# Moving the SBUF buffer of the weights' high parts by 384 bytes

## What is computed

```python
# first block, one layer
u = modulate(h, ...);  y = (silu(u @ w_gate) * (u @ w_up)) @ w_down   # d_ff 2816
h = layer_norm(ALPHA * h + 0.5 * gate * y)
u = modulate(h, ...);  y = hybrid_token_mixer(u, w_in, ...)          # conv, SSM, attention
h = layer_norm(ALPHA * h + gate * y)
... # the same feed-forward a second time, with other weights
# second block, one layer
z = rmsnorm(x) @ w_in;  ...                                          # attention, mLSTM
x = x + mixed @ w_out
u = relu(rmsnorm(x) @ w_ff1);  x = x + (u * u) @ w_ff2               # d_ff 4096
```

## Time and profile before

| | |
|---|---|
| median of 3 runs | 2522.7 us (2516.86 to 2528.89) |
| profiled execution | 2523.61 us |
| its span, first to last instruction | 2521.6 us |
| mean granted TensorE clock | 0.990 |
| PE, PEld, DVE, ACT, POOL busy | 97%, 92%, 74%, 51%, 43% |
| DMA | 481.35 MB, mean 191 GB/s |

### The profile page before, as it was taken

One profiled execution on the slowest core, in us unless ns is written; L12 is line 12 of the kernel. 1 busy time (PEld: TensorE's weight loads), 2 busy tenths in 40 slices (PEclk: granted clock), 3 DMA queues, 4 the chain that ended last, 5 costly groups with the idle time before them and its releaser, 6 DMA issues.

```text
span 2521.6 us, 52685 instructions
## 1 busy us (share of the span) xinstructions
PE 2448.4 (97%) x20017; PEld 2309.8 (92%) x20017; DVE 1872.2 (74%) x2869; ACT 1279.5 (51%) x2099; POOL 1077.4 (43%) x618
## 2 busy tenths in 40 slices
PE   7999999999999999999999999999999999999999
PEld 4999999878989989999998788999989999989999
DVE  5875999677687687679996777776856676756776
ACT  3445456356554454444553665544654544654544
POOL 3434987312043333369871110433650344740444
PEclk9999999899999999999999999999999999999999
DMA  9885864333477677767643235875434556534564
GB/s 365 302 287 186 276 222 135 114 106 104 151 279 255 191 261 277 251 233 243 201 135 101 93 101 191 285 256 170 138 123 143 171 188 191 169 103 149 172 188 133
DMA packets 131496, 481.35 MB, mean 191 GB/s; under 512 B 14848, under 2 KB 14848, under 8 KB 130560
## 3 DMA queue, kind: packets, MB, share of 16 engines
q1 hardware_dynamic: 106992, 388.49, 47.4%
q0 software_dynamic: 23040, 83.90, 9.1%
q10 hardware_dynamic: 1296, 6.64, 0.7%
HBM read 475.82 MB, written 3.15 MB: 190 GB/s over the span
## 4 chain that ended last, share of the span: by engine, by line
PE 71%; DVE 16%; DVEq 5%; ACT 3%; POOL 2%; issue 2%; DMA 1%; ACTq 0%; SPq 0%; POOLq 0%
PE ps L490 12%; PE ps L492 12%; PE ps L495 11%; PE ps L547 7%; DVE ps L1837 6%; PE ps L752 3%; PE ps L758 3%; PE ps L755 3%; DVEq L1847 2%; PE ps L480 2%; PE ps L481 2%; PE ps L482 2%; PE ps L703 2%; PE ps L525 2%; POOL eb L2232 2%
## 5 line engine op out<-in xcount | busy, mean ns | idle before, releaser
L1226 ACT ACTIVATE high<-ring 128x1024 fp32r<-128x1024 f32 x493 | 518.4, 1056 | 335.3 <-PE ps L495 192.7
L492 PE MATMUL ps<-u_parts,high 128*128 128x256 f32 x3680 | 499.3, 278 | 0.0
L492 PEld LDWEIGHTS ps<-u_parts,high 128*128 128x128 f32 x3680 | 458.6, 189 | 0.0
L2183 POOL TENSOR_TENSOR ring_parts<-ring,high 128x1024 fp32r<-128x1024 f32 x88 | 227.2, 2582 | 399.0 <-ACT high L1226 398.9
L2178 POOL TENSOR_TENSOR ring_parts<-ring,high 128x1024 fp32r<-128x1024 f32 x134 | 321.8, 2420 | 79.9 <-ACT high L1226 78.3
L1624 DVE TENSOR_TENSOR ring_parts<-ring,high 128x1024 fp32r<-128x1024 f32 x176 | 216.0, 1228 | 147.9 <-ACT high L1226 135.3
L2626 ACT ACTIVATE high<-ring 128x1024 fp32r<-128x1024 f32 x227 | 239.6, 1057 | 154.3 <-PE ps L547 67.4
L3166 POOL TENSOR_TENSOR ring_parts<-ring,high 128x1024 fp32r<-128x1024 f32 x66 | 159.1, 2410 | 327.7 <-ACT high L2626 327.7
L490 PE MATMUL ps<-ac_parts,high 128*128 128x256 f32 x1824 | 246.7, 278 | 5.1 <-ACT high L1226 5.1
L495 PE MATMUL ps<-ac_parts,ring_parts 128*128 128x256 f32 x1824 | 245.6, 277 | 0.0
L490 PEld LDWEIGHTS ps<-ac_parts,high 128*128 128x128 f32 x1824 | 226.1, 188 | 5.9 <-ACT high L1226 5.9
(11 more groups left out here) (534 smaller groups left out, 4981.6 us busy)
## 6 DMA issues: line engine op xcount, KB each, us to landing
ring<-stream_dram SPq DMA_DIRECT2D x736, 512.0 KB, 3.6
xc<-ada_dram POOLq DMA_DIRECT2D x84, 512.0 KB, 5.8
z<-ada_dram POOLq DMA_DIRECT2D x36, 512.0 KB, 7.3
qr<-ada_dram POOLq DMA_DIRECT2D x36, 512.0 KB, 7.5
h_aside<-ac ACTq DMA_DIRECT2D x2, 1024.0 KB, 4.2
eb<-ada_dram POOLq DMA_DIRECT2D x4, 512.0 KB, 5.5
h<-h_aside ACTq DMA_DIRECT2D x2, 1024.0 KB, 6.9
conb<-con_dram ACTq DMA_DIRECT2D x1, 1032.0 KB, 6.6
```

What stands on the lines that cost most here:

```text
L492: mm(out, hi[:, k * P:(k + 1) * P], xl[:, k], start=False, stop=False)
L1226: act(high_of(m, i), chunk_of(m, i), ACT.Copy).then_inc(made, 1)
L2183: nc.gpsimd.tensor_tensor(low_of(m, i), chunk_of(m, i), high_of(m, i), ALU.subtract)\
```

## The change

The buffer `high` is moved 384 bytes further from `ring` by 96 unused words ahead of it, and the unused words behind it grow from 48 to 80, so that everything that follows moves by exactly 512 bytes and keeps its place modulo 512. No instruction is added, removed or reordered, and no wait changes.

```diff
     m.ring, m.low = typed_twice("ring", RING * 1024)
+    def room(name, n):
+
+        sb(name, n)
+    room("past_ring", 96)
     m.high = sb("high", HIGH * 1024, F32R)
-    def room(name, n):
-
-        sb(name, n)
-    room("past_high", 48)
+    room("past_high", 80)
     h, hparts = typed_twice("h", ND * S)
```

More of the change, by code:

```diff
@@ L305, in memory @@
     m.ring, m.low = typed_twice("ring", RING * 1024)
-    m.high = sb("high", HIGH * 1024, F32R)
     def room(name, n):
         sb(name, n)
-    room("past_high", 48)
+    room("past_ring", 96)
+    m.high = sb("high", HIGH * 1024, F32R)
+    room("past_high", 80)
     h, hparts = typed_twice("h", ND * S)
```

## The result

The kernel after takes 2528.11 us (median of 22 runs, 2524.73 to 2531.14), the kernel before 2522.38 us in the same session (22 runs, 2516.70 to 2528.89). The ratio is 1.0022, with a 95% interval of 1.0014 to 1.0029: 5.7 us lost, between 3.5 and 7.3. That is inside the half per cent and inside the range, but on the other side of zero than the forecast of 2521. The profiled execution took 2527.03 us, 3.4 more than that of before.

What follows compares the result with a forecast made beforehand. PE was taken as the bound: number of matmuls times their spacing. From the profiled 2523.6 us, 2.1 (fourth place) and 0 ± 6.7 (hand-over) gave 2521.5, less 0.9 to the median, rounded to 2521 us; range 2506 to 2545.

Steps and rivals of the forecast that it cites:

- (b) The fourth place: Hidden layer's fourth place, both blocks: 16 of 24 matmuls leave distance 0 and gain 6.7 ns each, 2.1 us in all.
- The other end that I named: Fourth place of the hidden layer: 128 bytes are still too near, and nothing is gained.
- my second rival: First block falls into the slow rhythm, 16 steps in each of four passes: 19.9 us lost, 2541 us; chance 0.27.
- (c) The hand-over: Second block, L547 to L490, distance 0 to 128: gain 6.7 us if fast, loss 6.7 if slow; taken as 0.
- (a) The steady price of nothing: Products and downs on PE swapping distances 192 and 320: no cost, because both rhythms are seen at both distances.
- (d) DVE, ACT and POOL at nothing: Other engines, with `high` and chunk or ring at unequal places: no cost; POOL at most 22 us, taken as 0.
- nothing happens: Whole kernel: 192 and 320 cost the same, hand-over and fourth place may stay as they were; 2523 us, chance 0.12.
- the slow rhythm goes away: Both blocks: slow stretches turn fast once most overlaps at distance 0 are gone; 16.7 us gained, 2506 us, chance 0.18.

Runs made afterwards that it cites:

- The scan: Kernel before with the fourth place at 192; all buffers except ring and `high` at 64, 128, 256, 160, 224: ratios 1.0127, 1.0212, 1.0296, 1.0205, 1.0182.
- with 128 bytes: Kernel after with `high` moved 128 bytes instead of 384, the fourth place left where it was: 2530.87 us, ratio 1.0037 to the kernel before.
- the mirror image: Kernel before with the fourth place at 192, ring put at 384 from `high` instead of `high` at 384 from ring: 2525.53 us, ratio 1.0024.
- the down at 192: Kernel before with the fourth place at 192, the second block's hidden layer alone moved 384 bytes to place 64: 2524.38 us, ratio 1.0011.

## Why the prediction was wrong

**(b) The fourth place is the step that failed first.** I took 128 as far enough "because it is nearer to 192, where no cost is seen, than to 0" and booked a gain of 2.1 us. It measured a loss: the fourth place costs 120.0 ns at 128 and some 120 at 384, as at 0, and in the first block the slow rhythm stays behind it, 12 x 0.16 = 1.9 us. That is 4.0 us between the step and the chip. The scan shows why the argument was no good: the price doesn't rise from 192 towards 0 alone; a long stretch at 128 takes 118.7 ns, nearly as much as at 256. The other end that I named, that nothing is gained, was the right one, and the slow stretch behind it was in my second rival, but there it held for all 16 steps of a pass: it lasts two products. The price itself was read a little high: in the second block the step shows 2.86 against 2.72 us, 5.8 ns for each of 24 and not 6.7, which is 0.1 us in the sum.

**(c) The hand-over was mis-sized.** Half of the mechanism was there: slow and fast steps no longer took turns when its distance changed. The other half, that each layer then stays in one rhythm, failed: the rhythm turns twice inside every step, with 34 of 48 slow. I took 0, the middle of ± 6.7 us; it was + 3.0 us. That ± 6.7 covers it is no merit, because neither end of it happened. I hadn't asked what the two distances inside the down, 192 and then 320, would do.

**(a) The steady price of nothing** held where I looked for it, in the long stretch (1123 matmuls as before). Its reason, that both rhythms are found at 192 and at 320, is what the runs show too, but it doesn't carry the price: I took the two to be equally at home at both, and with all other buffers at 320 most of the first block is slow and the whole takes 1.0% longer. That the change is spared this by its order, because the products with low parts are still at 192, is an argument and was not tested alone. For it: a fast stretch stays fast, and slow ones turn fast at products with low parts, at L759 in the kernel after with the fourth place at 192, and at L496 of the second product behind the fourth place in the kernel after itself.

**(d) DVE, ACT and POOL at nothing** was right. L3119 has a median of 1212 ns, as before, and ACT and L2179 are as they were. POOL's L2184 did get longer, with a median of 2519 ns against 2407, and so it did with 128 bytes; with the fourth place at 192 it is at 2407 again. No engine waited for it.

Put together: 2520.6 + 2.1 (not gained) + 1.9 + 3.0 = 2527.6 us, against 2528.1 measured. The rival "nothing happens" is refuted by the loop, "the slow rhythm goes away" by its 34 of 48, and the first block fell into the slow rhythm for two products at a time only. That the time lies in the range and within half a per cent is in part luck: two small losses stand where one small gain was forecast.

**What stays open.** That places count modulo 256 bytes, and that distances 128, 160, 224 and 256 are dear when all other buffers stand at them, is shown. At 192 and at 64 both rhythms occur, the fast one more often at 192. Which rhythm a hand-over leaves behind is not explained: the loop is the same within some 0.1 us wherever places agree modulo 256, so in the second block the places decide it, but neither "64 is slow, 192 fast" (the mirror image) nor "a hand-over at distance 0 turns it" (the down at 192) covers all cases.

One rival stands in the second block. Apart from the fourth place, twelve kernels have distances of 64 and 192 modulo 256 alone. In the seven where ring and `high` are at equal places modulo 256 the loop takes 169.4 to 170.1 us; in the five where they are 128 apart it takes 170.8 to 172.4, wherever the hidden layer lies. So it may be the unequal places of the two buffers that cost there, or the change of distance inside a product that comes with them; no run parts the two. No version beat the kernel before by more than its interval; the nearest is the kernel before with the fourth place at 192 (0.9991).

## What to carry to other kernels

Where a kernel is bound by back-to-back matmuls, read their spacing from starts, by stage, and set it against the places of the two operands modulo 256 bytes: here the same matmul takes 113.3 to 120.0 ns, and 3% of the whole kernel hang on it. Give operands that stream together a distance that was measured to be good, seldom used slots too, and buffers that take turns as one operand equal places modulo 256; measure a distance before pricing it, because being far from a bad one is no evidence. Look at more than one stretch before a distance is called fast or slow. To size an effect of a few tenths of a per cent, compare the length of one loop between two named matmuls: here it repeats to some 0.1 us where the whole time spreads over 12.

## What was not expected of the hardware

The same 128 x 128 by 256 product has a spacing that hangs on the relative place of its two operands with a period of 256 bytes. At a granted clock of 1.00, long windows show 120.0 ns at 256, 118.7 at 128, 118.3 at 224 and 117.3 at 160; at 192, 64 and 320 stretches go at 113.3 or at 117.8, mostly fast at 192 and mostly slow in the first block at the other two. The Trainium skill (SBUF — State Buffer, "Who interferes with whom") gives PE two independent read ports and says that PE never waits on anyone. Taken as a rule for the spacing, it doesn't hold here: with all other buffers at 256 the kernel is 3.0% slower (1.0296), and its matmuls are 6.7 ns further apart. Whether it is the reading of the two operands that collides, the runs don't show; they show that their places count.
